# Memory key/value products moved between the first feed-forward products, and the end of the first group's second feed-forward in whole columns

## The chip, the cores and the metric

One Trainium2 chip, one core. The metric is the device time of one launch in microseconds (us). The kernel before has a median of 2804.96 us over three runs (2803.73 to 2806.08). The engines are called as the profile calls them: PE (TensorE matmul), PEld (its weight load), DVE (VectorE), ACT (ScalarE), POOL (GpSimd) and SP (SyncE, which here only issues the weight transfers).

## The reference, cut to what matters

One layer of an encoder over 1024 prompt rows and 32 sample rows, 1024 features wide, all in float32:

```
x = LN1(ALPHA*x + 0.5*SwiGLU_1(x))          # first feed-forward, 2816 hidden
x = LN2(ALPHA*x + W_mix_out[conv | sparse attention])
x = LN3(ALPHA*x + MemCrossAttn(x, mem_k, mem_v))
x = LN4(ALPHA*x + 0.5*SwiGLU_2(x))          # second feed-forward
mem_k = mem_prompt @ w_mem_k                # 256 memory tokens, also outputs
mem_v = mem_prompt @ w_mem_v
```

The sparse attention picks the best keys of each query by a score (up to 256 of 1024 for a prompt row). The memory's keys and values for the prompt are computed here; those of the sample come from a cache. They are first read in the cross-attention, long after the first feed-forward.

## The kernel before, in words

The rows are cut into two groups of 512 columns (activations lie feature-major, so a column is a token); the second group carries the 32 sample columns too. A float32 product is made of three float32r matmuls per 128 features: the high part of the weights with the high and the low part of the activations, and the low part of the weights with the high part (`linear`, L585 to L619).

**Weights.** `PLAN.weights` lists the 128-column weight tiles in the order of use. SP loads tile n (512 KB) into one of two raw buffers `WRAW`, once the low part of tile n-2 is made (L571 to L575). ACT makes the high part `WH` (`split_hi`, L915, L922), POOL the low part `WL` (`split_lo`, L1674, L1679), into a ring of four (`RING`). Tile n+4 is split when the last product of tile n is done. For the first twenty tiles DVE makes the low part instead of POOL (`first_lows`, L1330, L1336).

**Products.** A product (`Product`) is one weight tile times all columns of a group ("whole", 512 columns) or one half of them (256). Halves come in blocks of four weight tiles: four products on the first half, then the same four on the second; only the second time is a tile done and its place in the ring free. Products alternate between two PSUM slots; PE waits until the slot's last product was read (`product_read`).

**Segments.** `make_plan` writes the program as segments: load of group 0, memory key/value products (`memkv`), first feed-forward and mixing projection of group 0 ("chain"), index scores of group 0, load of group 1, the same chain of group 1, scores of group 1, attention of group 0, chain of group 0 (mixing output, memory attention, second feed-forward), attention of group 1, last chain of group 1. At the end of a segment every engine drains, and each waits for the others (`begin`): a barrier.

**Load** (L770 and L1169 to L1188). Token tiles of 128 rows are transposed on PE into one of two PSUM buffers `TR`; ACT copies each twice (high part `XH`, then ALPHA times into `Y`), DVE makes the low part. PE takes tile t+2 when DVE is done with t. Group 0's load begins with two tiles of the memory, into `HH` and `HL`.

**memkv** (L790 to L819, L1130, L1214). 16 products of 256 columns, one after the other; then 32 transposes for the two outputs, 16 and 8 for the cached memory keys and keys, ACT copies, and DMAs that the segment's end waits for.

**Feed-forward** (`ffn`, L188). In three parts of 6, 8 and 8 hidden tiles: gate and up products, then eight down products that add into `Y`. A whole down product is copied out of PSUM by ACT and added by POOL (L1092, L1759). The last part's down products are in halves, and DVE adds them out of PSUM (L1564, or L1384 where a norm follows). In group 0's second feed-forward DVE also holds `select` (L1342), the search for the best keys of group 1, from the ninth product on; the adds of L1564 stand behind it on DVE. Attention of group 1 needs its result.

Of the kernel before, what the change touches and what calls it, by code (L numbers as in the profile page):

```python
# [15 lines left out]
F32 = mybir.dt.float32  # L16
F32R = mybir.dt.float32r
# [4 lines left out]
P = 128  # L22
# [100 lines left out]
def load_tiles(g):  # L123
    rows0 = g.index * HALF
    memory = [("mem_prompt", t * P, P, t * P) for t in range(N_MEM // P)] if g.index == 0 else []
    return memory + [("x_sample", 0, rows, col) if rows == DEC else ("x_prompt", rows0 + col, rows, col)
                     for col, rows in g.tiles]
# [30 lines left out]
class Plan:  # L158
# [12 lines left out]
    def stage(self, name, g, tiles, nk, blocks, **facts):  # L171

        made, k = [], 0
        base = len(self.weights)
        self.weights += [(*src, nk) for src, _, _ in tiles]
        while k < len(tiles):
            halves = blocks(k)
            size = min(RING, len(tiles) - k) if halves else 1
            for half in (0, 1) if halves else (None,):
                for i in range(size):  # L180
                    src, j, more = tiles[k + i]
                    pr = self.add(base + k + i, name, j, g, half, nk, src[2])
# [5 lines left out]
    def ffn(self, which, g, after_norm, norm):  # L188
        made = []
        for part, (f0, nf) in enumerate(FFN_PARTS):  # L190
            tiles = [((f"ffn{which}_{kind}", P * f, P, 0), f, dict(kind=kind, f=f - f0, part=part))
                     for f in range(f0, f0 + nf) for kind in ("gate", "up")]
            split = part == 0 and after_norm is not None
            ups = self.stage("ffn", g, tiles, KD, lambda k: split and k < RING, which=which,
# [62 lines left out]
def make_plan():  # L257
# [4 lines left out]
    tiles = [((f"w_mem_{'kv'[j // KD]}", P * (j % KD), P, 0), j, {}) for j in range(2 * KD)]  # L262
    segments.append(("memkv", None, plan.stage("memkv", None, tiles, KD, lambda k: False)))

    def front(g, norm):
        ffn = plan.ffn(1, g, None, norm)
# [4 lines left out]
        if g.index == 1:  # L271
            ffn[0].mid.append(("select", 0))
        mix[14].end.append(("tokens",))
# [42 lines left out]

PLAN = make_plan()
# [12 lines left out]
LOAD_AT = {0: 0, 1: len(load_tiles(GROUPS[0]))}  # L330
# [3 lines left out]
FFN_AT = {(1, 0): 0, (1, 1): 1, (2, 0): 2, (2, 1): 3}  # L334
# [8 lines left out]
def encoder_step(nc, ins, outs):  # L343
    ctx = ExitStack()
    with ctx:
# [32 lines left out]
        KPA = place("KPA", [P, SEQ], F32, region(SEQ * 4))  # L378
# [3 lines left out]
        VP = place("VP", [P, 8, P], F32, region(SEQ * 4))  # L382
        VS = place("VS", [P, 5, P], F32, region(5 * P * 4))
# [38 lines left out]
        MKTOK = place("MKTOK", [P, 2, D], F32, r_a)  # L422
# [57 lines left out]
        back_done, back_hi, back_lo = sem("back_done"), sem("back_hi"), sem("back_lo")  # L480
        fwd_done, fwd_read = sem("fwd_done"), sem("fwd_read")
# [57 lines left out]

        def low_wait(engine, h, norm, j):  # L540
# [37 lines left out]
        def _(pe):  # L578
            def begin(s):
                if s:  # L580
                    pe.wait_ge(act_end, s)
                    pe.wait_ge(dve_end, s)
                    pe.wait_ge(pool_end, s)

            def linear(prs):  # L585
# [6 lines left out]
                hi, lo = (HH, HL) if lead.name in ("memkv", "mixout", "memo") or lead.kind == "down" else (XH, XL)  # L592
# [28 lines left out]
            def middle(pr):  # L621
                if pr.norm is not None and pr.j == 1:
                    pe.wait_ge(shift_source[pr.half], pr.norm + 1)
# [125 lines left out]

            def take_up(strand):  # L750
# [3 lines left out]
                elif kind == "memory":  # L754
                    memory_step(current[0], *what)
                elif kind == "tokens":
# [18 lines left out]
            def loads_of(b):  # L775
                return sum(1 for x in range(b + 1) if x % 4 == b % 4)

            current = [None]
            for s, (name, g, products) in enumerate(PLAN.segments):
# [10 lines left out]
                elif name == "memkv":  # L790
                    for pr in products:
                        linear([pr])
                    for k in range(4):
                        if k == 0:
                            pe.wait_ge(product_read[1], KD // 2)
                            pe.wait_ge(product_read[0], KD // 2)
                        if k == 2:
                            pe.wait_ge(product_read[1], KD)
                            pe.wait_ge(product_read[0], KD)
                            pe.wait_ge(pt_read, 1)  # L800
                        if k == 3:
                            pe.wait_ge(pt_read, 2)
                        src = MKT if k < 2 else MVT
                        for d in range(KD):
                            last = pe.transpose(TR[:, k % 2, d * P:(d + 1) * P], src[:, d, (k % 2) * P:(k % 2 + 1) * P],
                                                ident[:, :])
                        last.then_inc(pt_done, 1)
# [1022 lines left out]
```

## Time and profile before

| | us |
|---|---|
| median of three runs | 2804.96 |
| profiled execution | 2797.85 |
| its span | 2796.0 |
| PE busy in the span | 2562.9 |
| POOL busy | 1314.4 |
| DVE busy | 1020.6 |
| ACT busy | 938.7 |

PE is busy for 92% of the span. What is left is in a few places: the stretch before the first feed-forward, the norms and attention stages, and one long wait near the end of group 0's second feed-forward. The profiled execution lies 7.1 us under the median of the timed runs.

### The profile page before, as it was taken

The page shows a single profiled execution, that of the slowest core. Times are in us where ns is not written, and L with a number is a line of the kernel's source. Part 1 is how long each engine was busy: PE and PEld are TensorE (multiplying, and loading weights), DVE is VectorE, ACT ScalarE, POOL GpSimd, SP SyncE. Part 2 cuts the span into 40 slices and gives each one's busy share as a digit, 9 for nine tenths or more (in the row PEclk, how much of TensorE's full clock was granted, in tenths as well). Part 3 has the DMA queues.
Part 4 walks back from the last instruction along what each step waited for, and adds up shares of the span by engine and source line. Part 5 has one row for each costly group of instructions (what it writes and reads, how often), then busy time and mean ns, then how long its engine had stood idle before and what let it go on. Part 6 is the DMA issues. An engine that isn't in the chain of part 4 may idle for free.

```text
span 2796.0 us, 40502 instructions
## 1 busy us (share of the span) xinstructions
PE 2562.9 (92%) x16397; PEld 2284.5 (82%) x16397; DVE 1020.6 (37%) x1973; ACT 938.7 (34%) x1594; POOL 1314.4 (47%) x805
## 2 busy tenths in 40 slices
PE   5799999896999998897989899995799899999997
PEld 5678889775999998894489888884656898999997
DVE  2100002325720006038463678888254636100003
ACT  3333333323333223227434333331154343333230
POOL 0166665532666655340052577663200525666662
PEclk8899999998999999997799999998789999999999
DMA  5433332334233222334022233331210222333331
GB/s 160 142 90 98 98 91 77 97 92 145 78 97 91 84 83 58 105 84 129 35 61 61 61 91 101 113 97 53 91 65 31 61 61 61 116 104 98 99 86 60
DMA packets 420111, 245.09 MB, mean 88 GB/s; under 512 B 22816, under 2 KB 410976, under 8 KB 418656
## 3 DMA queue, kind: packets, MB, share of 16 engines
q1 hardware_dynamic: 389088, 195.65, 24.5%
q10 hardware_dynamic: 26480, 23.21, 2.7%
q0 software_dynamic: 4368, 23.73, 2.3%
q8 instruction: 131, 2.15, 0.3%
q14 instruction: 44, 0.36, 0.0%
HBM read 218.79 MB, written 21.74 MB: 86 GB/s over the span
## 4 chain that ended last, share of the span: by engine, by line
PE 72%; DVE 11%; DVEq 5%; issue 4%; DMA 3%; ACT 3%; POOL 1%; ACTq 1%; POOLq 0%; SPq 0%
PE LIN L610 61%; DVE M L1347 5%; DVEq L1350 4%; PE LIN L853 3%; PE TR L866 2%; PE TR L880 2%; DVE SC L1349 1%; DVE Y L1443 1%; PE LIN L685 1%; PE TR L661 1%; DMA WRAW<-in_w_mem_v 1%; ACT WH L922 1%; PE LIN L835 1%; DMA WRAW<-in_w_mem_k 1%; DMA spill_cl<-YCL 1%
## 5 line engine op out<-in xcount | busy, mean ns | idle before, releaser
L1679 POOL TENSOR_TENSOR WL<-WRAW,WH 128x1024 fp32r<-128x1024 f32 (+1 forms) x362 | 849.7, 2348 | 659.0 <-ACT WH L922 652.5
L610 PE MATMUL LIN<-XH,WH 128*128 128x256 f32 (+3 forms) x2984 | 829.1, 323 | 61.1 <-DVE Y L1386 25.2
L610 PE MATMUL LIN<-XH,WL 128*128 128x256 f32 (+3 forms) x2984 | 821.2, 320 | 0.0
L610 PE MATMUL LIN<-XL,WH 128*128 128x256 f32 (+3 forms) x2984 | 819.8, 320 | 0.0
L610 PEld LDWEIGHTS LIN<-XH,WH 128*128 128x128 f32 (+1 forms) x2984 | 523.9, 191 | 103.7 <-issue 49.8
L610 PE MATMUL LIN<-HH,WH 128*128 128x256 f32 (+2 forms) x1824 | 515.6, 303 | 75.4 <-DVE Y L1564 46.3
L610 PEld LDWEIGHTS LIN<-XL,WH 128*128 128x128 f32 (+1 forms) x2984 | 524.7, 191 | 37.5
L610 PEld LDWEIGHTS LIN<-XH,WL 128*128 128x128 f32 (+1 forms) x2984 | 522.1, 191 | 36.5
L610 PE MATMUL LIN<-HL,WH 128*128 128x256 f32 (+2 forms) x1824 | 513.5, 301 | 0.0
L610 PE MATMUL LIN<-HH,WL 128*128 128x256 f32 (+2 forms) x1824 | 512.3, 301 | 0.0
L922 ACT ACTIVATE WH<-WRAW 128x1024 fp32r<-128x1024 f32 (+2 forms) x382 | 392.9, 1030 | 238.9 <-PE LIN L610 135.3
L610 PEld LDWEIGHTS LIN<-HH,WH 128*128 128x128 f32 x1824 | 336.2, 191 | 90.4 <-issue 66.4
L926 ACT ACTIVATE FG<-LIN 128x512 f32<-128x512 f32 (+3 forms) x248 | 148.1, 598 | 758.0 <-PE LIN L610 756.4
L610 PEld LDWEIGHTS LIN<-HL,WH 128*128 128x128 f32 x1824 | 335.9, 191 | 10.2
L610 PEld LDWEIGHTS LIN<-HH,WL 128*128 128x128 f32 x1824 | 334.4, 190 | 9.8
L1384 DVE TENSOR_TENSOR Y<-LIN,Y 128x256 f32<-128x256 f32 (+1 forms) x32 | 13.8, 431 | 635.4 <-PE LIN L610 595.2
L1749 POOL TENSOR_TENSOR FP<-FG 128x512 f32<-128x512 f32 (+3 forms) x92 | 117.7, 1280 | 208.2 <-ACT FG L926 208.2
L1347 DVE MAX8 M<-SC 128x8 f32<-128x384 f32 (+6 forms) x209 | 183.9, 880 | 71.5 <-issue 71.5
L1349 DVE MATCH_REPLACE8 SC<-M,SC 128x384 f32<-128x384 f32 (+6 forms) x209 | 180.4, 863 | 1.9 <-issue 0.3
L1751 POOL TENSOR_TENSOR HL<-FP,HH 128x512 fp32r<-128x512 f32 (+3 forms) x92 | 117.5, 1277 | 67.7 <-ACT HH L1087 67.7
L1759 POOL TENSOR_TENSOR Y<-FG,Y 128x512 f32<-128x512 f32 (+1 forms) x64 | 85.1, 1330 | 83.4 <-ACT FG L926 83.1
L1744 POOL TENSOR_TENSOR CSUM<-Y 128x256 f32<-128x256 f32 (+1 forms) x12 | 9.0, 754 | 231.0 <-DVE Y L1391 231.0
(185 smaller groups left out, 2006.4 us busy)
## 6 DMA issues: line engine op xcount, KB each, us to landing
WRAW<-in_ffn_gate SPq DMA_DIRECT2D x88, 512.0 KB, 3.8
WRAW<-in_ffn_up SPq DMA_DIRECT2D x88, 512.0 KB, 3.8
WRAW<-in_ffn_down SPq DMA_DIRECT2D x64, 512.0 KB, 3.9
WRAW<-in_w_mix_in SPq DMA_DIRECT2D x44, 512.0 KB, 3.8
WRAW<-in_ffn_down SPq DMA_DIRECT2D x32, 384.0 KB, 3.4
WRAW<-in_w_mix_out SPq DMA_DIRECT2D x16, 512.0 KB, 3.9
WRAW<-in_w_mem_q SPq DMA_DIRECT2D x16, 512.0 KB, 3.9
WRAW<-in_w_mem_o SPq DMA_DIRECT2D x16, 512.0 KB, 3.9
```

The lines of the kernel that those rows point to most:

```text
L610: last = pe.matmul(LIN[0:pr.rows, pr.slot, out:out + w], wt[:, pr.tile % RING, c, 0:pr.rows], x[:, c, col:col + w], start=(c == 0 and wt i ...
L853: last = pe.matmul(LIN[0:rows, a % 2, k0:k0 + w], (QA1 if g.sample else QA0)[lo:lo + 64, h // 2, col:col + rows], kmat[lo:lo + 64, k0:k0 + ...
L866: last = pe.transpose(TR[0:w, 0, at_ + kb:at_ + kb + rows], PR[0:rows, a % 4, kb:kb + w], ident[0:rows, 0:rows])
L922: act.activation(WH[:, n % RING, 0:nk, 0:width], WRAW[:, n % 2, 0:nk, 0:width], ACT.Copy).then_inc(hi_split, 1)
L926: return act.activation(dst, in_psum(pr), func, scale=scale)
L1347: dve.max(M8[0:rows, :], sc)
L1349: dve.match_replace(sc, M8[0:rows, :], sc, TAKEN)
L1350: dve.drain()
L1679: pool.tensor_tensor(WL[:, n % RING, 0:nk, 0:width], WRAW[:, n % 2, 0:nk, 0:width], WH[:, n % RING, 0:nk, 0:width].bitcast(F32), ALU.subtr ...
L1749: pool.tensor_tensor(FP_[:, cols(pr)], FG[:, 0, cols(pr)], FG[:, 1, cols(pr)], ALU.mult).then_inc(multiplied, 1)
L1751: pool.tensor_tensor(HL[:, pr.f, cols(pr)], FP_[:, cols(pr)], HH[:, pr.f, cols(pr)].bitcast(F32), ALU.subtract).then_inc(hidden_lo, 1)
L1759: pool.tensor_tensor(Y[:, pr.j, cols(pr)], FG[:, pr.j % 2, cols(pr)], Y[:, pr.j, cols(pr)], ALU.add)\
```

## The change

**Plan.** The memkv segment is gone. `ffn` takes a list `between`: in group 0's first feed-forward, one memory product stands behind every second whole product, its weight tile at the same place in the weight list. All 16 lie in the first 32 whole products (gate/up and down of part 0, gate/up of part 1). The first four weight tiles of this feed-forward are now taken in halves. The load of group 0 holds its four token tiles alone; the two memory tiles are transposed behind the third and fourth product, into new tiles `MH` and `ML`. The transposes of the outputs and of the caches stand behind products of part 1's down stage and the next gate. There is no barrier between the load of group 0 and its chain (`JOINED`).

**Load.** ACT copies the high part first; the copy into `Y` (`residual_of`) of tile t follows the high part of tile t+1, and PE takes tile t+2 when both the low part and this copy of tile t are done. This holds for group 1's load too.

**End.** `halves = final and (norm is not None or g.sample)`: the last down products of group 0's second feed-forward are whole, copied by ACT and added by POOL.

```diff
@@ stage @@
+            whole += not halves
+            if between and not halves and whole % 2 == 0:
+                j = between.pop(0)
+                self.weights.append((f"w_mem_{'kv'[j // KD]}", P * (j % KD), P, 0, KD))
+                made.append(self.add(len(self.weights) - 1, "memkv", j, None, None, KD))
@@ ffn @@
-            split = part == 0 and after_norm is not None
+            split = part == 0 and (after_norm is not None or between)
...
+            halves = final and (norm is not None or g.sample)
-            downs = self.stage("ffn", g, tiles, nf, lambda k: final, which=which,
+            downs = self.stage("ffn", g, tiles, nf, lambda k: halves, between, which=which,
                                norm=norm if final else None)
@@ make_plan, front @@
+            ffn[2].end.append(("memory tokens", 0))
+            ffn[3].end.append(("memory tokens", 1))
+            last = max(k for k, pr in enumerate(ffn) if pr.name == "memkv")
+            for k in range(4):
+                ffn[last + 1 + k].end.append(("memory turn", k))
+            for k in range(2):
+                ffn[last + 7 + k].end.append(("cached memory", k))
+            ffn[last + 9].end.append(("cached keys",))
@@ barriers @@
+JOINED = [1]
+        def barriers(s):
+            return sum(1 for k in range(1, s + 1) if k not in JOINED)
@@ PE, linear @@
+                if lead.name == "memkv":
+                    hi, lo = MH, ML
+                    if lead.j == 0:
+                        pe.wait_ge(back_lo, LOAD_AT[1])
+                if lead.p < 2 * RING and lead.first or lead.p == RING:
+                    pe.wait_ge(back_lo, 2 * lead.half + 2)
@@ PE, to_feature @@
                     pe.wait_ge(back_lo, b - 1)
+                    pe.wait_ge(residual, tokens_before(b - 1))
@@ ACT @@
-                act.activation(XH[:, :, col:col + rows], src, ACT.Copy)
-                act.activation(Y[:, :, col:col + rows], src, ACT.Copy, scale=ALPHA).then_inc(back_hi, 1)
+                act.activation(hi[:, :, col:col + rows], src, ACT.Copy).then_inc(back_hi, 1)
+
+            def residual_of(b, col, rows):
+                act.wait_ge(back_lo, b + 1)
+                src = TR[:, b % 2, :].rearrange("p (d t) -> p d t", d=KD)[:, :, 0:rows]
+                act.activation(Y[:, :, col:col + rows], src, ACT.Copy, scale=ALPHA).then_inc(residual, 1)
...
+            def memory_turn(k):
+                act.wait_ge(pt_done, k + 1)
+                act.activation((MKTOK if k < 2 else MV)[:, k % 2, :], TR[:, k % 2, :], ACT.Copy).then_inc(pt_read, 1)
...
+                if k == 3:
+                    all_moved()
+                    act.dma_start(CMK[:, :, :], ins["cache_mem_k"][0, 0].rearrange("(b p) h d -> p b (h d)", p=P))\
+                        .then_inc(ck_loaded, 16)
...
                     for t, (src, _, rows, col) in enumerate(tiles):
-                        from_feature(LOAD_AT[g.index] + t, col, rows, src == "mem_prompt")
+                        from_feature(LOAD_AT[g.index] + t, col, rows, XH)
...
+                        if s == 0 and t < RING - 1:
+                            split_hi(t)
+                        if t >= 1:
+                            residual_of(LOAD_AT[g.index] + t - 1, tiles[t - 1][3], tiles[t - 1][2])
+                        if s == 0 and t >= 2:
+                            load_memory(t - 2)
```

Where instructions move, in the order of each engine's queue. The first place is ACT at the start of the program, before; `TR` is PSUM after a transpose, `WRAW` a raw weight tile, the names in brackets are the semaphores that an instruction waits for:

```order
L1175 DMA XT<-in_mem_prompt 128x1024 x2
L1175 DMA XT<-in_x_prompt 128x1024 x2
L922 ACTIVATE WH<-WRAW 128x1024 [waits raw_loaded0]
L922 ACTIVATE WH<-WRAW 128x1024 [waits raw_loaded1]
L932 ACTIVATE HH<-TR 128x8x128 [waits back_done]
L1175 DMA XT<-in_x_prompt 128x1024
L932 ACTIVATE HH<-TR 128x8x128 [waits back_done]
L1175 DMA XT<-in_x_prompt 128x1024
L934 ACTIVATE XH<-TR 128x8x128 [waits back_done]
L935 ACTIVATE Y<-TR 128x8x128
```

And now:

```order
L1266 DMA XT<-in_x_prompt 128x1024 x4
L981 ACTIVATE XH<-TR 128x8x128 [waits back_done]
L972 ACTIVATE WH<-WRAW 128x1024 [waits raw_loaded0]
L981 ACTIVATE XH<-TR 128x8x128 [waits back_done]
L972 ACTIVATE WH<-WRAW 128x1024 [waits raw_loaded1]
L986 ACTIVATE Y<-TR 128x8x128 [waits back_lo]
L981 ACTIVATE XH<-TR 128x8x128 [waits back_done]
L972 ACTIVATE WH<-WRAW 128x1024 [waits raw_loaded0]
L986 ACTIVATE Y<-TR 128x8x128 [waits back_lo]
L990 DMA XT<-in_mem_prompt 128x1024
L981 ACTIVATE XH<-TR 128x8x128 [waits back_done]
```

The group's own tiles come first, a weight split stands between them, and the copy into `Y` comes one tile later. The second place is ACT inside group 0's first feed-forward as it is now, around the first memory products (`FG` takes a gate or up product, `MKT` a memory product):

```order
L976 ACTIVATE FG<-LIN 128x512 [waits product]
L1180 ACTIVATE HH<-FP 128x512 [waits multiplied]
L972 ACTIVATE WH<-WRAW 128x1024 [waits product,raw_loaded1]
L976 ACTIVATE MKT<-LIN 128x256 [waits product]
L972 ACTIVATE WH<-WRAW 128x1024 [waits product,raw_loaded0]
L976 ACTIVATE FG<-LIN 128x512 [waits product]
```

Before, the `MKT` copies stood in a row of their own ahead of the first `FG`. The third place is DVE at the end of group 0's second feed-forward, before; `SC` holds the scores of `select`, and L1640 is the first instruction of group 1's attention:

```order
L1347 MAX M_126<-SC 32x8
L1349 MATCH_REPLACE SC<-M_126,SC 32x544
L1351 TENSOR_SCALAR SC<-SC 32x544
L1564 TENSOR_TENSOR Y<-LIN,Y 128x256 [waits product,added]
L1564 TENSOR_TENSOR Y<-LIN,Y 128x256 [waits product] x3
L1564 TENSOR_TENSOR Y<-LIN,Y 128x256 [waits product,added]
L1564 TENSOR_TENSOR Y<-LIN,Y 128x256 [waits product] x11
L1640 ISA PR,NM<-LIN,SC 128x640 [waits pool_end,s_done,act_end,pe_end]
```

And now:

```order
L1427 TENSOR_SCALAR SC<-SC 32x544
L1714 ISA PR,NM<-LIN,SC 128x640 [waits pool_end,s_done,act_end,pe_end]
L1714 ISA NM 128x1
L1714 ISA PR,NM<-LIN,SC 128x640 [waits s_done]
L1714 ISA NM 128x1
```

The sixteen adds are gone from DVE; eight adds of 512 columns stand on POOL instead, each ahead of a weight split.

## Rows read from the trace of the kernel before

**Rows 1.** The page's head: the span.
```profile
span 2796.0 us, 40502 instructions
```
**Rows 2.** Chain of waits, first 130 us: start, duration, what.
```profile
37.26 8.02 PE LIN L610 x48
...
99.43 3.19 PE TR L805 x16
...
107.25 0.11 PE TR L817
...
114.84 15.32 PE LIN L610 x54
```
**Rows 3.** Timeline from 0 us: start, duration, instruction, idle before and releaser.
```profile
5.59 1.94 PE L771 MATMUL TR<-ident,XT 128*128 128x128 f32 x8 [5.59 <-DMA XT<-in_mem_prompt]
6.41 1.06 ACT L922 ACTIVATE WH<-WRAW 128x1024 fp32r<-128x1024 f32 x1 [1.94 <-DMA WRAW<-in_w_mem_k]
...
8.71 1.97 PE L771 MATMUL TR<-ident,XT 128*128 128x128 f32 x8 [1.18 <-DMA XT<-in_mem_prompt]
11.94 1.06 ACT L922 ACTIVATE WH<-WRAW 128x1024 fp32r<-128x1024 f32 x1 [4.47 <-DMA WRAW<-in_w_mem_k]
```
**Rows 4.** Chain of waits over the whole span.
```profile
188.58 253.16 PE LIN L610 x1089
...
449.50 2.86 PE LIN L610 x24
...
2018.05 2.48 PE LIN L853 x4
```
**Rows 5.** Groups by line and shape: count, busy, mean ns, idle before.
```profile
L1679 POOL TENSOR_TENSOR WL<-WRAW,WH 128x1024 fp32r<-128x1024 f32 x328 | 787.4, 2402 | 652.0 <-ACT WH L922 646.1
...
L1759 POOL TENSOR_TENSOR Y<-FG,Y 128x512 f32<-128x512 f32 x32 | 41.5, 1296 | 36.2 <-ACT FG L926 36.2
```
**Rows 6.** DMA issues, first 120 us: count, size, median us to landing.
```profile
WRAW<-in_w_mem_v SPq DMA_DIRECT2D x8, 512.0 KB, 5.9
...
WRAW<-in_ffn_gate SPq DMA_DIRECT2D x3, 512.0 KB, 3.9
...
CMK<-in_cache_mem_k ACTq DMA_DIRECT2D x1, 1024.0 KB, 7.8
...
out_mem_v<-MV ACTq DMA_DIRECT2D x1, 1024.0 KB, 6.2
```
**Rows 7.** Timeline of the load of group 1.
```profile
673.28 1.23 DVE L1327 TENSOR_TENSOR XL<-TR,XH 128x1024 fp32r<-128x1024 f32 x1 [9.57 <-ACT Y L935]
...
674.66 1.07 PE L771 MATMUL TR<-ident,XT 128*128 128x128 f32 x8 [1.77 <-DVE XL L1327]
...
681.69 0.79 PE L610 MATMUL LIN<-XH,WH 128*128 128x256 f32 x2 [1.55 <-DVEq L1664]
```
**Rows 8.** Timeline of PE, end of group 0's second feed-forward.
```profile
1917.05 0.28 PE L610 MATMUL LIN<-HH,WH 128*128 128x256 f32 x1
...
1971.00 0.55 PE L610 MATMUL LIN<-HH,WH 128*128 128x256 f32 x1 [46.25 <-DVE Y L1564]
```
**Rows 9.** Timeline of DVE in the same place.
```profile
1899.27 1.23 DVE L1347 MAX8 M<-SC 128x8 f32<-128x1024 f32 x1 [0.34 <-issue]
1902.19 1.23 DVE L1347 MAX8 M<-SC 128x8 f32<-128x1024 f32 x1 [0.34 <-issue]
...
1931.47 1.23 DVE L1347 MAX8 M<-SC 128x8 f32<-128x1024 f32 x1 [0.34 <-issue]
1934.40 1.23 DVE L1347 MAX8 M<-SC 128x8 f32<-128x1024 f32 x1 [0.34 <-issue]
...
1970.09 0.43 DVE L1351 TENSOR_SCALAR SC<-SC 32x544 f32<-32x544 f32 x1 [0.23 <-issue]
```
**Rows 10.** Timeline of POOL in the same place.
```profile
1899.05 2.41 POOL L1679 TENSOR_TENSOR WL<-WRAW,WH 128x1024 fp32r<-128x1024 f32 x1
...
2015.40 2.34 POOL L1679 TENSOR_TENSOR WL<-WRAW,WH 128x1024 fp32r<-128x1024 f32 x1 [0.51 <-ACT WH L922]
```

More of the change, by code:

```diff
@@ L124, in load_tiles @@
     rows0 = g.index * HALF
-    memory = [("mem_prompt", t * P, P, t * P) for t in range(N_MEM // P)] if g.index == 0 else []
-    return memory + [("x_sample", 0, rows, col) if rows == DEC else ("x_prompt", rows0 + col, rows, col)
-                     for col, rows in g.tiles]
+    return [("x_sample", 0, rows, col) if rows == DEC else ("x_prompt", rows0 + col, rows, col)
+            for col, rows in g.tiles]
 class Product:
@@ L169, in add, with stage @@
         return pr
[L171 to L175, printed above, removed]
+    def stage(self, name, g, tiles, nk, blocks, between=(), **facts):
+        made, k, whole = [], 0, 0
         while k < len(tiles):
@@ L178, in stage @@
             size = min(RING, len(tiles) - k) if halves else 1
+            base = len(self.weights)
+            self.weights += [(*src, nk) for src, _, _ in tiles[k:k + size]]
             for half in (0, 1) if halves else (None,):
@@ L185, in stage, with ffn @@
             k += size
+            whole += not halves
[3 more added lines that the diff above has]
+                made.append(self.add(len(self.weights) - 1, "memkv", j, None, None, KD))
         return made
-    def ffn(self, which, g, after_norm, norm):
+    def ffn(self, which, g, after_norm, norm, between=()):
         made = []
@@ L192, in ffn @@
                      for f in range(f0, f0 + nf) for kind in ("gate", "up")]
-            split = part == 0 and after_norm is not None
-            ups = self.stage("ffn", g, tiles, KD, lambda k: split and k < RING, which=which,
+            split = part == 0 and (after_norm is not None or between)
+            ups = self.stage("ffn", g, tiles, KD, lambda k: split and k < RING, between, which=which,
                              after_norm=after_norm if split else None)
@@ L261, in make_plan @@
     segments.append(("load", g0, []))
-    tiles = [((f"w_mem_{'kv'[j // KD]}", P * (j % KD), P, 0), j, {}) for j in range(2 * KD)]
-    segments.append(("memkv", None, plan.stage("memkv", None, tiles, KD, lambda k: False)))
     def front(g, norm):
-        ffn = plan.ffn(1, g, None, norm)
+        ffn = plan.ffn(1, g, None, norm, list(range(2 * KD)) if g.index == 0 else [])
         tiles = [(("w_mix_in", c0, m, 0), j, dict(kind=kind, f=i)) for j, (kind, i, c0, m) in enumerate(MIX_TILES)]
@@ L755, in take_up @@
                     memory_step(current[0], *what)
+                elif kind == "memory tokens":
+                    b = MEM_AT + what[0]
+                    pe.wait_ge(xt_loaded[b % 4], 16 * loads_of(b))
+                    to_feature(b, P, b % 4)
+                elif kind == "memory turn":
+                    memory_turn(*what)
+                elif kind == "cached memory":
+                    cached_memory(*what)
+                elif kind == "cached keys":
+                    cached_keys()
                 elif kind == "tokens":
@@ L1059, in take_up @@
                     memory_step(current[0], *what)
+                elif kind == "memory tokens":
+                    b = MEM_AT + what[0]
+                    from_feature(b, what[0] * P, P, MH)
+                elif kind == "memory turn":
+                    memory_turn(*what)
+                elif kind == "cached memory":
+                    cached_memory(*what)
+                elif kind == "cached keys":
+                    cached_keys()
                 elif kind == "tokens":
@@ L1505, in take_up @@
                     memory_step(current[0], *what)
+                elif kind == "memory tokens":
+                    low(MEM_AT + what[0], what[0] * P, P, MH, ML)
                 elif kind == "select":
@@ L1571, in _ @@
                     for t, (src, _, rows, col) in enumerate(load_tiles(g)):
[L1572 to L1577 removed]
+                        low(LOAD_AT[g.index] + t, col, rows, XH, XL)
+                        if s == 0:
+                            first_lows(t + 1)
+                elif name == "chain":
                     for prs in paired(products):
```

197 lines of the change are left out of this document (96 added, 101 removed).

## The prediction

> **What bounds the kernel now.** I read the head of the page first: a span of 2796.0 us [rows 1], PE nearly always busy. So PE's time counts where it works, and elsewhere the wait that ends last. The chain of waits shows what a product costs at full pace: 24 matmuls of 256 columns take 2.86 us, and 1089 of mostly 512 columns take 253.16 us, 0.2325 us each, so 5.57 us for a whole product of 24 [rows 4]. Two products on two halves thus cost 5.72 us against 5.57 us.
>
> Two stretches are not at that pace. The first is the start. The chain begins the first feed-forward only at 114.84 us [rows 2]. Ahead of it stand six transposed tiles, 16 memory products from 37.26 us until shortly before the transposes at 99.43 us (some 62 us for 16 x 2.86 = 45.8 us of matmuls, since each weight tile is awaited: in this stretch one takes 5.9 us to land, ACT 1.06 us, DVE 1.23 us), and transposes and stores from 99.43 us on [rows 2, 3, 6, 7].
>
> The second is the end of group 0's second feed-forward. PE starts its last down products at 1917.05 us, has done two by 1924.7 us, and then waits 46.25 us for an add on DVE [rows 8]. That add stands behind the key search, whose last instruction starts at 1970.09 us [rows 9]. After it the other fourteen half products run, and then POOL still has splits to make until 2015.40 + 2.34 = 2017.74 us [rows 10]: the last four products finish four weight tiles 2.86 us apart, but two raw buffers with a landing between do not split them that fast. Group 1's attention begins at 2018.05 us [rows 4].
>
> **The start, step by step.** Now PE meets its first product as soon as four token tiles are transposed. Tile 0 is transposed by 5.59 + 1.94 = 7.53 us, tile 1 by 8.71 + 1.97 = 10.68 us [rows 3]; I keep both, as the same two raw weight tiles and four token tiles are requested at first. ACT then works in the order shown above, at about 0.95 us for each of its operations of 1024 columns (1.06 us long, overlapping a little). High part of tile 1 until 11.7; second weight, which landed at 11.94 [rows 3], split until 13.0; copy of tile 0 into Y until 13.9. This copy is a wait that is new: PE may overwrite the PSUM buffer only after it, so tile 2 is transposed from 14.0 to 16.0 us. High part until 17.0; split of the third weight (its raw buffer was free at 9.5 + 1.23 = 10.8 us, landing 3.9 to 5.9 us later [rows 6], so it is there) until 18.0; copy of tile 1 until 18.9; tile 3 transposed until 21.0 us. The first product starts at 21.0 us. Bounds: 17 us if ACT's work overlaps more, 28 us if the third weight lands ten microseconds late.
>
> A first product after idling is slow: 54 matmuls take 15.32 us where 12.6 us are due, a loss of 2.8 us, and the first two memory products take 8.02 us for 5.72 us, 2.3 us lost [rows 2]. The new start pays one such loss in place of the other. So the feed-forward is ahead by (114.84 + 2.8) - (21.0 + 2.3) = 94.3 us. From this go:
> - 16 memory products at 2.86 us: 45.8 us. Nothing hides them, PE is the bound here.
> - 72 transposes (16 of the memory tiles, 32 of the outputs, 24 of the caches) at 0.11 us, the price in the chain at 107.25 us [rows 2], 7.9 us, and about 1 us for starting seven sets. At the price at 99.43 us (3.19 us for 16, [rows 2]) they would be 14.4 us; these came after short waits, so I take the lower one.
> - four weight tiles in halves: 4 x (5.72 - 5.57) = 0.6 us.
> - stalls while the small loads compete for DMA: 1 us, an estimate, bounded by 0 and the first rival below.
>
> That leaves 94.3 - 45.8 - 8.9 - 0.6 - 1.0 = 38.0 us of gain.
>
> What is costed at nothing here: the weights' low parts of the memory products, now 2.40 us on POOL in place of 1.23 us on DVE. Two whole products and a memory product take PE 14.0 us; POOL has 3 x 2.40 + 1.30 + 1.30 = 9.8 us of it [rows 5]: the two at 1.30 us are down adds, and multiply and split of a hidden tile have the same size. Without that cover each group would cost the difference. ACT stops at the fourth turn until both stores have landed (6.2 us [rows 6]) and holds its PSUM copies and splits behind it; PE has two products, 11.1 us, before it needs the slot. The cache's load (7.8 us [rows 6]) is issued only then, 6.2 + 7.8 + 1.5 = 15.5 us after the fourth turn, against three products, 16.7 us: hidden by 1.2 us, which is thin, but a miss costs a microsecond or two, once.
>
> **Load of group 1.** Here the new order costs time. PE may take tile t+2 only after tile t's copy into Y, and this follows the high part of tile t+1; each further tile is then a serial loop of transposes (1.07 us [rows 7], up to the 1.94 us of rows 3) and two ACT copies (1.9 us). Starting from the same first tile, I get high part 0 until 672.2, copy 0 until 674.9, tile 2 transposed until 676.1, copy 1 until 678.1, tile 3 until 679.7, copy 2 until 681.7, the 32-row tile until 682.8, the last two copies until 684.5, and the first product at 684.7 in place of 681.69 us [rows 7]: 3.0 us lost. Bounds 0 (all overlaps) to 5 us.
>
> **The whole-column end.** From 1917.05 us eight products of 5.57 us run without DVE: to 1961.7 us. Two half products took 1924.75 - 1917.05 = 7.7 us for 5.72 us of work, so PE stood 2.0 us for the last hidden tile; a whole product needs that tile only after seven eighths of 5.57 us, 2.4 us later than a half one, and this stall goes. POOL adds 1.30 and splits 2.40 us per product [rows 5], 3.7 us in 5.57 us, and is done about 4.5 us after PE, at 1966.2 us. What is late next is the key search itself, until 1970.09 + 0.43 = 1970.5 us [rows 9], and the barrier: attention can start at 1970.7 us in place of 2018.05 us [rows 4], a gain of 47.3 us. Bounds: 40 us if POOL's queue runs over, 47.5 us if not.
>
> One rule speaks against it. The search now has POOL's work beside it for another 44 us. The rows show one round at 1899.27 to 1902.19 us, while POOL splits a tile, in 2.92 us, and one at 1931.47 to 1934.40 us, with POOL idle, in 2.93 us [rows 9, 10]. The Trainium skill ("SBUF — State Buffer", section "Who interferes with whom") says that VectorE and GpSimd share a port pair: a VectorE instruction with two SBUF inputs and a GpSimd instruction that reads SBUF block each other, one with a single input does not. By the blocking half of the rule the search would be held by POOL; by the single-input half it is free, and the trace agrees with the latter.
>
> **The sum.** 38.0 - 3.0 + 47.3 = 82.3 us. The profiled execution of 2797.85 us would become 2715.5 us. It is 7.1 us faster than the median of the timed runs, so I take the difference from the median: 2804.96 - 82.3 = 2722.7, forecast 2722 us.
>
> **Rivals.**
> - *The weight ring starves between the memory products.* Each group of three weight tiles needs 1.5 turns of each raw buffer. A turn is landing + 1.06 + 2.40 us, and up to 1.3 us of POOL's other work. At a landing of 3.9 us that is 1.5 x 8.7 = 13.0 us, under 14.0 us; at 5.9 us in all groups [rows 6] it is 1.5 x 10.7 = 16.0 us, 2 us more in each of 16 groups: 2722 + 32 = 2754 us. For it: the cache and constant loads that went with 5.9 us move along. Against: they touch a few groups, and the plain landing beside feed-forward weights is 3.9 us.
> - *POOL's reads hold up the search.* Eight adds and splits, 8 x 3.7 = 29.6 us, all on DVE's time: attention at 2000.3 us, 2752 us in all. Against it: the equal rounds above.
> - *The start does not move,* because the third weight or a token tile arrives as late as before and PE begins near 37 us: 16 us less, 2738 us.
> - *Slower.* The first rival, at its extreme: the ring decides the first feed-forward wholly. The gain of 82 us is gone when each of 16 groups loses 5.2 us, at a landing of (14.0 + 5.2)/1.5 - 4.8 = 8.0 us for every tile; at 10 us it would be 1.5 x 14.8 = 22.2 us a group, 131 us, 2853 us. The slowest load in these rows is 7.8 us, and that is for twice the bytes.
>
> **Chances.** Forecast 0.83, starved ring 0.06, held search 0.03, late start 0.06, slower 0.02. The forecast's own spread is the sum of its terms' bounds: a start at 17 to 28 us, 5.5 us of transposes, 2 us of group 1's load, 7 us at the end, some 10 us down and 15 us up. The range takes in the late start and half of the way to the other two: 2709 to 2741 us. Within 0.2% (5.6 us, about what timing can tell from no change) 0.01, slower 0.02, faster 0.97.
>
> **What would show it.** In the profile after: the first 256-column product near 21 us; 24-matmul memory products between whole ones with no idle PE time in front; the first norm of group 0 some 38 us earlier; the first product of group 1 three microseconds later after its first transposes; no PE wait of tens of microseconds before the last down products, PE idle some 9 us before attention, and DVE's search as the last to end there. I would be wrong if PE waits for weight splits between memory products, if the search's rounds lengthen beside POOL's adds, or if POOL ends that segment.

## The result and the profile after

The changed kernel takes 2711.84 us (median of 4 runs, 2711.0 to 2716.24) against 2804.69 us (4 runs, 2803.73 to 2806.08) on the same chip: a ratio of 0.9672, 95% interval 0.9655 to 0.9688. The forecast was 2722 us, with a range of 2709 to 2741 us. It was right in sign and inside its range, and 10 us too slow.

The profiled execution of the changed kernel took 2712.45 us, its span is below; against that of before [rows 1] it is 85.5 us shorter, where the sum of the prediction was 82.3 us.

Head of the page of the changed kernel:

```profile
span 2710.5 us, 40319 instructions
```

The start. The chain of waits of the changed kernel, from its beginning (start, duration, what):

```profile
13.26 0.92 ACT Y L986
...
14.31 1.95 PE TR L846 x8
...
18.26 0.92 ACT Y L986
...
19.32 1.94 PE TR L846 x8
21.25 9.87 PE LIN L645 x72
...
35.72 229.92 PE LIN L645 x1224
265.64 0.87 PE TR L796 x8
266.51 5.57 PE LIN L645 x24
...
407.66 2.86 PE LIN L645 x24
```

Where [rows 2] had PE on the memory's products until about 99 us, the feed-forward now begins at 21 us. The copies into Y (L986) do delay the third and fourth tile, as the prediction had it. From 35.72 us PE runs 1224 matmuls in one piece, memory products among them: no weight is awaited. The set of transposes after it takes 0.87 us, and the next product follows at once; so do the others. The last line, the first 24 matmuls behind the first norm's products, is the same piece of work as the row at 449.50 us of [rows 4]: 41.8 us earlier. What PE waited for between 20 and 460 us in the changed kernel (line <- releaser: us in total, times, longest) says the same; the memory products do not appear in it:

```profile
PE LIN L645 <- DVE Y L1460: 5.7, 1, 5.7
PE LIN L645 <- POOL HL L1826: 1.6, 1, 1.6
```

The load of group 1, on PE (timeline of the changed kernel):

```profile
627.35 3.65 PE L846 MATMUL TR<-ident,XT 128*128 128x128 f32 x16 [8.32 <-POOLq L1876]
633.12 1.07 PE L846 MATMUL TR<-ident,XT 128*128 128x128 f32 x8 [2.12 <-ACT Y L986]
636.31 1.94 PE L846 MATMUL TR<-ident,XT 128*128 128x128 f32 x8 [2.12 <-ACT Y L986]
...
643.09 0.82 PE L645 MATMUL LIN<-XH,WH 128*128 128x256 f32 x2 [1.70 <-ACTq L1380]
```

From the third tile on each now waits 2.12 us for the copy into Y, where [rows 7] waited 1.77 us or less for the low part. First transposes to first product are 643.09 - 627.35 = 15.74 us; in the kernel before they were 681.69 - 669.24 = 12.45 us, from this row to the last of [rows 7]:

```profile
669.24 3.65 PE L771 MATMUL TR<-ident,XT 128*128 128x128 f32 x16 [8.32 <-POOLq L1800]
```

The end of group 0's second feed-forward, on PE, POOL and DVE (three timelines of the changed kernel):

```profile
1929.51 4.18 PE L902 MATMUL LIN<-KPA,QA 64*128 64x512 f32 x6 [4.76 <-DVEq L1739]
```

```profile
1925.52 1.26 POOL L1834 TENSOR_TENSOR Y<-FG,Y 128x512 f32<-128x512 f32 x1 [1.92 <-ACT FG L976]
1926.75 2.34 POOL L1754 TENSOR_TENSOR WL<-WRAW,WH 128x1024 fp32r<-128x1024 f32 x1
```

```profile
1926.68 0.72 DVE L1423 MAX8 M<-SC 32x8 f32<-32x544 f32 x1 [0.34 <-issue]
...
1928.47 0.91 DVE L1427 TENSOR_SCALAR SC<-SC 32x544 f32<-32x544 f32 x1 [0.23 <-issue]
```

The 46 us wait of [rows 8] is gone. PE stands 4.76 us before the attention, and what it awaits is the search on DVE, done at 1929.38 us. But POOL is done at 1929.09 us, only 0.3 us earlier; the prediction had given it 4 us.

By stage, from the rows above and their counterparts in the trace before:

| place | before, us | after, us | ahead by |
|---|---|---|---|
| 24 matmuls behind the first norm's products | 449.50 | 407.66 | 41.8 |
| first product of group 1 | 681.69 | 643.09 | 38.6 |
| first round of group 1's search | 1606.22 | 1569.15 | 37.1 |
| end of that search | 1970.52 | 1929.38 | 41.1 |
| first product of group 1's attention | 2018.05 | 1929.51 | 88.5 |
| first product after that attention | 2149.01 | 2064.62 | 84.4 |
| span | 2796.0 | 2710.5 | 85.5 |

So the barrier itself gave 47.4 us, as predicted. Two lines hold what was not: the search became 4 us shorter, and group 1's attention 4 us longer.

### The profile page after: what moved, and what is told of

Its sections match the earlier page's. It is cut to its first block, busy times and chain, and to the rows that moved or that the text cites. A ratio compares the mean times of both kernels' runs of the same rounds, so it can differ in the third digit from the quotient of the medians.

```text
span 2710.5 us, 40319 instructions
## 1 busy us (share of the span) xinstructions
PE 2553.4 (94%) x16301; PEld 2270.4 (84%) x16301; DVE 995.9 (37%) x1941; ACT 944.0 (35%) x1608; POOL 1362.5 (50%) x833
## 4 chain that ended last, share of the span: by engine, by line
PE 75%; DVE 10%; DVEq 6%; issue 3%; ACT 2%; DMA 1%; POOL 1%; ACTq 1%; POOLq 0%; SPq 0%
PE LIN L645 63%; DVEq L1426 5%; DVE M L1423 5%; PE LIN L902 3%; PE TR L915 2%; PE TR L929 2%; DVE Y L1519 1%; PE LIN L722 1%; PE TR L698 1%; DMA spill_cl<-YCL 1%; DVE Y L1514 1%; PE LIN L884 1%; POOL WL L1754 1%; DVEq L1422 1%; PE TR L846 0%
## 5 line engine op out<-in xcount | busy, mean ns | idle before, releaser
L645 PE MATMUL LIN<-XH,WH 128*128 128x256 f32 (+4 forms) x3016 | 834.5, 321 | 55.2 <-DVE Y L1462 25.3
L645 PE MATMUL LIN<-XH,WL 128*128 128x256 f32 (+4 forms) x3016 | 826.3, 318 | 0.0
L645 PE MATMUL LIN<-XL,WH 128*128 128x256 f32 (+4 forms) x3016 | 825.1, 318 | 0.0
L645 PE MATMUL LIN<-HH,WH 128*128 128x256 f32 (+2 forms) x1632 | 465.3, 307 | 8.5 <-POOL HL L1826 6.8
L645 PE MATMUL LIN<-HL,WH 128*128 128x256 f32 (+2 forms) x1632 | 462.9, 306 | 0.0
L645 PE MATMUL LIN<-HH,WL 128*128 128x256 f32 (+2 forms) x1632 | 462.2, 305 | 0.0
L645 PEld LDWEIGHTS LIN<-HH,WH 128*128 128x128 f32 x1632 | 296.1, 189 | 23.9 <-POOL HL L1826 8.3
L645 PEld LDWEIGHTS LIN<-HL,WH 128*128 128x128 f32 x1632 | 296.0, 189 | 12.6
L1824 POOL TENSOR_TENSOR FP<-FG 128x544 f32<-128x544 f32 (+3 forms) x94 | 117.9, 1254 | 221.6 <-ACT FG L976 221.6
L1826 POOL TENSOR_TENSOR HL<-FP,HH 128x544 fp32r<-128x544 f32 (+3 forms) x94 | 118.0, 1255 | 68.3 <-ACT HH L1180 68.3
```

The source lines that it names most:

```text
L645: last = pe.matmul(LIN[0:pr.rows, pr.slot, out:out + w], wt[:, pr.tile % RING, c, 0:pr.rows], x[:, c, col:col + w], start=(c == 0 and wt i ...
L1824: pool.tensor_tensor(FP_[:, cols(pr)], FG[:, 0, cols(pr)], FG[:, 1, cols(pr)], ALU.mult).then_inc(multiplied, 1)
L1826: pool.tensor_tensor(HL[:, pr.f, cols(pr)], FP_[:, cols(pr)], HH[:, pr.f, cols(pr)].bitcast(F32), ALU.subtract).then_inc(hidden_lo, 1)
```

## Experiments

All ratios are to the kernel before, timed on the same chip in the same session (2799.93 us, 9 runs, for the first four; 2803.98 us, 7 runs, for the last three).

**The end alone.** The kernel before, with the whole-column end:

```
-            downs = self.stage("ffn", g, tiles, nf, lambda k: final, which=which,
+            halves = final and (norm is not None or g.sample)
+            downs = self.stage("ffn", g, tiles, nf, lambda k: halves, which=which,
...
-FFN_AT = {(1, 0): 0, (1, 1): 1, (2, 0): 2, (2, 1): 3}
+ADDED_AT = {(1, 0): 0, (1, 1): 2 * KD, (2, 0): 4 * KD, (2, 1): 7 * KD}
...
```

> The kernel before with one part of the change: the last down products of group 0's second feed-forward are whole, copied by ACT and added by POOL. Theory (DVE's key search held PE; its end now sets the barrier): the 46 us wait of PE goes, attention of group 1 starts right behind the search, about 47 us earlier than at 2018.05 us, so about 2757 us. Rival (POOL's adds, splits or the barrier take the wait's place): POOL ends this segment some microseconds behind the search and the gain stays under 42 us, above 2763 us. Rival (the parts are not independent, the end needs the moved start): under 30 us.

Measured: 2748.28 us, ratio 0.9816 (0.9795 to 0.9836), 51.6 us less than before; its four runs spread from 2743.6 to 2752.3 us. Timelines of DVE (search of the 640 keys, and its end) and PE in this kernel:

```profile
1605.51 0.83 DVE L1348 MAX8 M<-SC 128x8 f32<-128x640 f32 x1 [0.44 <-issue]
1606.41 0.09 DVE L1350 MATCH_VALUE_LOAD SC<-M,SC 128x8 f32 x1
1606.56 0.82 DVE L1350 MATCH_REPLACE8 SC<-M,SC 128x640 f32<-128x640 f32 x1
1607.81 0.83 DVE L1348 MAX8 M<-SC 128x8 f32<-128x640 f32 x1 [0.42 <-issue]
...
1965.49 0.43 DVE L1352 TENSOR_SCALAR SC<-SC 32x544 f32<-32x544 f32 x1 [0.23 <-issue]
```

```profile
1966.06 2.25 PE L854 MATMUL LIN<-KPA,QA 64*128 64x512 f32 x3 [9.83 <-DVEq L1665]
```

PE stands 9.8 us in front of the attention, near the 9 us predicted, and the attention begins 0.1 us after the search, where before it began 47.5 us after it. POOL is done at 1960.56 us, 5.4 us before the search. By these rows the edit gives 47.4 us, and this half of the change does what the prediction said: the search and the barrier are what remains. In this execution the search had also begun 5.6 us earlier than before, without an edit ahead of it; the granted clock of the first 1600 us was 0.95 against 0.94, and how much of the 5.6 us that explains is not shown.

**The start alone.** The changed kernel, with the half products at the end:

```
-            halves = final and (norm is not None or g.sample)
+            halves = final
...
-ADDED_AT = {(1, 0): 0, (1, 1): 2 * KD, (2, 0): 4 * KD, (2, 1): 7 * KD}
+ADDED_AT = {(1, 0): 0, (1, 1): 2 * KD, (2, 0): 4 * KD, (2, 1): 6 * KD}
```

> The changed kernel with its last down products of group 0's second feed-forward in halves again, added by DVE. Theory: the first feed-forward's gain of about 42 us and the loss of about 3 us in group 1's load stay, the 46 us wait behind the search is back. If the search's rounds of 640 keys, which took 2.30 us in the kernel before and 2.13 us in the changed one, depend on where their loop lies in DVE's program (it lies here as in the changed kernel), the search is 5 us shorter here too: about 42 us gain, 2762 us. If they depend on the whole-column end beside them, the rounds are back at 2.30 us: about 37 us gain, 2767 us.

Measured: 2758.23 us, ratio 0.9855 (0.9835 to 0.9875), a gain of 41.7 us. Its timeline of PE shows the old end again, with a wait 5.5 us shorter than before:

```profile
1929.35 0.55 PE L645 MATMUL LIN<-HH,WH 128*128 128x256 f32 x1 [40.75 <-DVE Y L1642]
```

The two halves add up to 93.3 us, the whole change gave 92.9 us. Each of these gains is known to about 5 us to either side, so this shows that the halves do not get in each other's way by more than several microseconds; smaller effects, which the profiles show below, may cancel in it.

**The place of a loop.** The search's instructions are the same in all these kernels, but the rounds over 640 keys took 2.297 us in the kernel before and in the end alone, and 2.129 us in the changed kernel and in the start alone, with nothing else on DVE. The rows of the changed kernel's DVE beside those of the end alone above:

```profile
1573.43 0.83 DVE L1423 MAX8 M<-SC 128x8 f32<-128x640 f32 x1 [0.35 <-issue]
1574.33 0.09 DVE L1425 MATCH_VALUE_LOAD SC<-M,SC 128x8 f32 x1
1574.41 0.81 DVE L1425 MATCH_REPLACE8 SC<-M,SC 128x640 f32<-128x640 f32 x1
1575.56 0.83 DVE L1423 MAX8 M<-SC 128x8 f32<-128x640 f32 x1 [0.34 <-issue]
```

The instructions take the same time; the gaps between them differ, 0.42 against 0.34 us in front of MAX8, and some 0.06 us ahead of the MATCH_REPLACE8. What the change moves is the loop's place in DVE's program: counted in the program of each kernel as it is built, without branch labels, the first MAX8 of the 640-key loop is instruction 1086 of DVE before and 1064 after. Four empty instructions were put ahead of the searches in the changed kernel, which brings the 896-key loop from 1082 to 1086:

```
+                    if what[0] == 1:
+                        for _ in range(4):
+                            dve.drain()
                     select(GROUPS[what[0]])
```

> The changed kernel with four more DVE drains ahead of the search of group 1's keys, which move its five loops by four instructions; the loop over 896 keys then lies at the instruction numbers at which the loop over 640 keys lay in the kernel before. Theory (place of a loop in the program): the rounds of 896 keys take some 0.17 us more, 2.80 us, the other four loops are as they were, the search ends 5 us later and attention of group 1 with it, time up by about 5 us, 2717 us. Rival (the slow rounds came from their operands or from work beside them): all rounds as in the changed kernel, time the same within 1 us.

Measured: 2717.49 us, ratio 0.9699 (0.9684 to 0.9714). The DVE of this kernel:

```profile
1730.78 1.09 DVE L1423 MAX8 M<-SC 128x8 f32<-128x896 f32 x1 [0.42 <-issue]
...
1733.60 1.09 DVE L1423 MAX8 M<-SC 128x8 f32<-128x896 f32 x1 [0.42 <-issue]
```

An 896-key round now takes 2.832 us; in the changed kernel it took 2.632. All other loops keep their pace, and the search ends at 1935.16 us, 5.8 us later than in the changed kernel (1.1 us of it because it began later), with the attention behind it. The medians differ by 5.6 us, but their ratios to before overlap; it is the rounds that decide. So in both cases the loop that starts at instruction 1086 is the slow one, over 640 keys or over 896; that the changed kernel has none there is worth 32 x 0.168 = 5.4 us to it. Why that place is slow stays open. The Trainium skill ("Runtime: NRT & Kernel Launch", section "Instruction fetch mechanics") says that a branch whose target is not in the window of fetched instructions forces a transfer before the engine goes on. If every slow round did that, instruction transfers would show once a round; in the kernel before, between 1610 and 1676 us (28 rounds), the DMA view has three, of all engines together (packets, MB, share of the engines):

```profile
q8 instruction: 3, 0.05, 0.3%
```

So it is not that rule, in that form.

**The load of group 1 in its old order.** The changed kernel, with the copy into Y directly behind the high part in group 1's load, and PE no longer waiting for it by itself:

```
-                    pe.wait_ge(residual, tokens_before(b - 1))
+                    if b < LOAD_AT[1]:
+                        pe.wait_ge(residual, tokens_before(b - 1))
...
-                        from_feature(LOAD_AT[g.index] + t, col, rows, XH)
+                        if s:
...
+                            act.activation(XH[:, :, col:col + rows], both, ACT.Copy)
+                            act.activation(Y[:, :, col:col + rows], both, ACT.Copy, scale=ALPHA).then_inc(back_hi, 1)
+                        else:
+                            from_feature(LOAD_AT[g.index] + t, col, rows, XH)
...
```

> The changed kernel with the load of group 1 in the old order: high part, copy into Y, then DVE's low part, and PE waits for the low part alone. Theory (the copy that follows one tile later makes the loop serial): the first product of group 1 stands 12.5 us behind its first transposes instead of 15.7 us, time 3 us lower, about 2709 us. Rival (the 3 us come from the clock or from later transposes, not from the order): no change.

Measured: 2709.6 us, ratio 0.9677 (0.9664 to 0.969). PE in this kernel:

```profile
623.73 3.65 PE L847 MATMUL TR<-ident,XT 128*128 128x128 f32 x16 [7.39 <-POOLq L1884]
629.14 1.07 PE L847 MATMUL TR<-ident,XT 128*128 128x128 f32 x8 [1.77 <-DVE XL L1411]
...
636.36 0.80 PE L645 MATMUL LIN<-XH,WH 128*128 128x256 f32 x2 [1.74 <-DVEq L1747]
```

The stage takes 12.63 us again in place of 15.74, 3.1 us less: the term of 3.0 us is the order of ACT's two copies. The medians differ by 2.2 us; their ratios to before overlap, so a timing alone does not tell these two kernels apart.

**Weights of the memory products: more of them.** The changed kernel, with a memory product behind every whole product:

```
-            if between and not halves and whole % 2 == 0:
+            if between and not halves and whole % 1 == 0:
```

> The changed kernel with a memory product behind every whole product of the first feed-forward in place of every second one. Theory (the weight ring has slack between the memory products): one whole and one memory product take TensorE 5.57 + 2.86 = 8.43 us and need two weight tiles, one turn of each raw buffer; a turn is landing 3.9 + high part 1.06 + low part 2.40 = 7.4 us, up to 8.7 us with an addition on GpSimd. So no stall that a timing could tell: the changed kernel's 2711.8 us within 3 us, no idle TensorE in front of the memory products. Rival (the ring starves where the small loads raise the landing to 5.9 us): a turn is 9.4 to 10.7 us, 1 to 2.3 us lost in each of 16 groups, 2728 to 2748 us.

Measured: 2714.24 us, ratio 0.9686 (0.9663 to 0.9709), the changed kernel's time within 3 us. A piece of this kernel's chain, and one of PE's waits between 20 and 460 us:

```profile
35.95 104.14 PE LIN L645 x624
```

```profile
PE LIN L645 <- ACT FG L976: 0.4, 1, 0.4
```

Up to 140.09 us PE does nothing but products. Then the chain leaves it and goes round in weight transfers and splits until 157.54 us, where PE has waited 0.4 us: ACT copied a gate or up product out of PSUM late, since it stood behind a split whose weight had not landed. That is the only wait for weights, so two weight tiles per 8.43 us are about as many as the ring gives. The change asks for three in 14.0 us, and none of its waits is for a weight: the starved-ring rival is refuted for it.

**All of them in a row.** Here the 16 memory products stand together behind the second whole product:

```
-            if between and not halves and whole % 2 == 0:
+            while between and not halves and whole >= 2:
```

> The changed kernel with all 16 memory products in a row, behind the second whole product of the first feed-forward, so that nothing stands between them. Theory (standing between whole products is what hides the supply of their weights): in a row each takes TensorE 2.86 us, while the two raw buffers give a tile every 7.4 / 2 = 3.7 us, so 16 x 0.84 = 13.4 us less about 3 us for the tiles split in advance, some 10 us lost: 2722 us, with TensorE waiting for the low part of a weight in front of most of them. If the landing is 5.9 us, a tile every 4.7 us, 29 us less the stock: 2738 us. Rival (where they stand is of no account, only that the first feed-forward starts early): 2712 us.

Measured: 2728.35 us, ratio 0.9733 (0.9711 to 0.9756), 16.5 us more than the changed kernel, where 10 were expected. The chain of this kernel has left PE and goes round in the weights:

```profile
82.36 4.39 DMA WRAW<-in_w_mem_v
...
86.77 1.07 ACT WH L972
...
87.91 2.40 POOL WL L1754
...
90.32 4.69 DMA WRAW<-in_w_mem_v
```

One turn of a raw buffer is 90.32 - 82.36 = 8.0 us (7.7 to 8.3 in the turns around it), so a tile every 4.0 us against 2.86 us of matmuls: 16 x 1.14 = 18 us, less the stock. The theory has the rate of the ring right; the landing was 4.1 to 4.7 us and not the 3.9 us that was assumed. Where PE stands it has wrong: not in front of the low part of a weight, but in ten waits, 9.0 us in all, for ACT's copies of earlier memory products out of PSUM, which stand behind the split that awaits its weight (PE's waits between 20 and 460 us):

```profile
PE LIN L645 <- ACT MVT L976: 5.3, 6, 1.4
PE LIN L645 <- ACT MKT L976: 3.7, 4, 1.4
```

The first norm's products begin 13.2 us later than in the changed kernel (417.17 against 403.98 us). So standing between whole products is worth 13 us by the profile, 16 by the medians, of the start's gain.

**A shorter search.** The changed kernel, with 13 rounds in place of 17 for the 32-row tile:

```
-    return [(t, 128, 128 * (5 + t), 32) for t in range(4)] + [(4, DEC, SKEYS, (SKEYS // 4) // 8)]
+    return [(t, 128, 128 * (5 + t), 32) for t in range(4)] + [(4, DEC, SKEYS, (SKEYS // 4) // 8 - 4)]
```

> The changed kernel with 13 rounds in place of 17 in the search for the best keys of the 32-row tile, so that some of that tile's best keys are not marked (that part of the result changes). The search on VectorE then ends 4 x 1.90 = 7.6 us earlier, near 1921.8 us. Theory (the last weight split on GpSimd, done at 1929.09 us, is only 0.3 us from setting the barrier itself): attention of the second group starts within 0.5 us of where it did, 2711.5 us in all. Rival (GpSimd has 4 us to spare, as the prediction had it): attention 4 us or more earlier, 2707 to 2704 us.

Measured: 2714.23 us, ratio 0.9684 (0.9662 to 0.9705): no gain. Timelines of DVE, POOL and PE in this kernel:

```profile
1922.26 0.68 DVE L1427 TENSOR_SCALAR SC<-SC 32x544 f32<-32x544 f32 x1 [0.23 <-issue]
```

```profile
1922.60 2.60 POOL L1754 TENSOR_TENSOR WL<-WRAW,WH 128x1024 fp32r<-128x1024 f32 x1
...
1928.15 2.34 POOL L1754 TENSOR_TENSOR WL<-WRAW,WH 128x1024 fp32r<-128x1024 f32 x1
```

```profile
1930.78 2.04 PE L902 MATMUL LIN<-KPA,QA 64*128 64x512 f32 x2 [4.63 <-POOLq L1876]
```

The search is done 7.5 us before POOL, PE now waits for POOL, and the attention starts 360.2 us after the search's first round (1570.59 us here), where it was 360.4 us in the changed kernel. The 7.6 us are worth 0.2. In the changed kernel the two tie.

## Why the prediction was right, and where its sizes were off

**The start: 38.0 us predicted, 41.8 us measured.** The first product starts at 20.91 us in the timeline (21.0 predicted). The other terms were each a little too dark: the 72 matmuls from 20.91 to 31.12 us take 10.2 us where 8.6 are due, so the cold start cost 1.6 us and not 2.3; a set of eight transposes takes 0.87 us with nothing around it, 9 x 0.87 = 7.8 us in place of 8.9; the 1 us for stalls by small loads did not come. That is 117.6 - 22.5 - 45.8 - 7.8 - 0.6 = 40.9 us. Of the rest, 0.6 us is a wait for a hidden tile that is gone, most likely hidden by a product between (two such waits, 2.2 us, between 115 and 500 us before; one of 1.6 us after, and two again, 3.2 us, with the memory products in a row); 0.3 us stay open. The low parts on POOL, the stores and the cache's load cost nothing, as assumed.

**The load of group 1: 3.0 us predicted, 3.3 us measured,** and 3.1 us came back with the old order.

**The end: 47.3 us predicted, 47.4 us measured** (search's end to attention, 47.53 us before, 0.13 us after). Right in size; the statement on what stands beside it was wrong in part. In the end alone POOL has the slack that the working gave it (4.3 us from 1966.2 to 1970.5; 5.4 measured). In the whole change it has 0.3 us, because the search became shorter: it is that term which the prediction left at zero.

**The search: 0 predicted, 4.1 us measured.** The prediction took the search's end relative to its beginning from the trace before. The loop over 640 keys moved in DVE's program, and its 32 rounds became 5.4 us shorter. Those over 896 keys, which moved too, went from 2.661 to 2.632 us a round, another 0.9 us, whose cause was not tried. The instructions between and behind the loops took 2.2 us back. POOL's work did not lengthen the rounds: one of 1024 keys takes 2.93 us in both kernels, and one of the 32-row tile, beside which POOL was idle before and works now, 1.90 us in both. It did lengthen the single instruction behind some of the loops, TENSOR_SCALAR: the last took 0.43 us with POOL idle [rows 9] and takes 0.91 us beside POOL's split. The Trainium skill ("SBUF — State Buffer", section "Who interferes with whom") names that operation among those that can take the port pair shared with GpSimd, in the perf modes that use two ports, and excepts these modes from what it says of a single input; the prediction overlooked that when it went by the number of inputs alone. The trace agrees, and where the DVE instruction came first it was POOL's split that grew, to 2.60 us, in the shorter search above.

**Attention of group 1: 0 predicted, 4.1 us lost.** It lasts 131.0 us before and in the end alone, 132.4 us with the start alone, and 135.1 to 135.2 us in the changed kernel and the five others. Views by window of the kernel before and of the changed one (duration, busy time of PE, PEld, DVE, ACT and POOL, granted clock, DMA share, GB/s):

```profile
2042.00:2136.00 94.00, 93.58 (x505) 51.73 (x502) 53.80 (x122) 56.21 (x95) 0.00 (x0) 1.00 0.00 1
2136.00:2149.00 13.00, 10.24 (x94) 6.22 (x93) 7.83 (x25) 7.17 (x28) 0.00 (x0) 0.83 0.01 2
```

```profile
1953.50:2048.00 94.50, 94.08 (x504) 52.17 (x501) 53.23 (x120) 55.55 (x93) 0.00 (x0) 0.99 0.00 1
2048.00:2064.60 16.60, 14.08 (x95) 7.78 (x94) 8.41 (x27) 7.60 (x30) 0.00 (x0) 0.61 0.00 0
```

The same 94 or 95 matmuls of the 32-row tile at the end take 16.6 us at a mean granted clock of 0.61, where they took 13.0 us at 0.83: the clock falls from its upper to its lower level (1.00 to 0.50) earlier, some 122 us into the stage where it was some 126 us before. The work ahead of it in the stage and its waits are alike. What in the changed kernel brings the fall forward was not tried; since it is the same in six kernels, it is unlikely to be chance. PE's idle time in front of the stage is not the cause by itself: 9.83 us in the end alone go with 131.0 us, 9.86 us in the kernel with the four empty instructions with 135.2 us.

That these two terms of 4.1 us, neither of them foreseen, cancel is luck: without the shorter search the profile would have gained 81.4 us, without the longer attention 89.6 us.

**The median.** Profile to profile the gain is 85.5 us, 3.2 us over the sum: 3.8 from the start, 4.1 from the search, 0.1 from the barrier, less 0.3, less 4.1 in the attention, less 0.4 elsewhere (1.5 us lost between 643 and 1569 us, 1.1 us gained after 2065). The other 7 us of the 10 come from the base: the prediction took the sum from the median, 2804.96 us, though the profiled execution it was made against took 2797.85. Before, single runs spread from 2795.8 to 2808.5 us over three sessions, and the profiled one lay low. Taken from the profiled execution the forecast would have been 2715.5 us. Where in the kernel before its longer runs spent these 7 us is not shown, since only one execution of it was profiled; in the later sessions the longest of them has the lowest granted clock over the span (0.942 at 2808.5 us, 0.946 at 2795.8 us).

Of the rivals, the starved ring is refuted by the chain and by the denser order, the late start by the row at 21.25 us, and the held search by its rounds. Its weak form, half a microsecond to one at the end of some loops, is there.

## What to carry to other kernels

Small products whose weights arrive more slowly than they are consumed can be put between large ones whose weights arrive early: here PE lost nothing with them spread, and 13 to 16 us with them in a row. A wait in front of a barrier is worth the whole distance to the next late engine, but look for the next two: when the search became shorter by accident, POOL was already there. And make the sum and its base from the same execution: the 7 us between profile and median of the kernel before were more than the 3.2 us that the errors of the terms left in the sum.

## What was not expected of the hardware

- A short loop on DVE costs 0.17 to 0.20 us more per round (2.297 against 2.129 us, 2.832 against 2.632 us) when its first instruction is number 1086 of that engine's program as built; loops that start at 1064, 1068, 1073, 1077, 1082, 1091, 1095, 1100, 1104, 1113 and 1122 do not show it (the largest other difference is 0.03 us, 896 keys at 1104 against 1082). Four empty instructions ahead of it moved the cost from one loop to another.
- TENSOR_SCALAR on DVE and POOL's operations take turns, and the one that begins first goes on. Behind the 640-key loop of the kernel before, DVE began 0.05 us ahead; its instruction took 0.50 us, and POOL's split grew from 1.85 to 2.16 us (DVE, then POOL):

```profile
1679.54 0.50 DVE L1351 TENSOR_SCALAR SC<-SC 128x640 f32<-128x640 f32 x1 [0.23 <-issue]
```

```profile
1675.40 1.85 POOL L1679 TENSOR_TENSOR WL<-WRAW,WH 128x768 fp32r<-128x768 f32 x1
...
1679.59 2.16 POOL L1679 TENSOR_TENSOR WL<-WRAW,WH 128x768 fp32r<-128x768 f32 x1
```

  In the changed kernel POOL began 0.07 us ahead, with an addition of 1.30 us, and DVE took 1.58 us, of which 1.23 lie beside it (DVE, then POOL):

```profile
1637.17 1.58 DVE L1427 TENSOR_SCALAR SC<-SC 128x640 f32<-128x640 f32 x1 [0.23 <-issue]
```

```profile
1637.10 1.30 POOL L1834 TENSOR_TENSOR Y<-FG,Y 128x512 f32<-128x512 f32 x1 [1.07 <-ACT FG L976]
```

  MAX8 and MATCH_REPLACE8 beside the same operations do not change: a round of the 32-row tile takes 1.903 us with POOL idle and 1.904 us beside its adds and splits.
- The same attention stage took 131.0 or 135.2 us by the kernel around it, through the granted clock of its last 13 to 17 us.
